# First attention: probabilities times values in split float32r passes, with turned probability tiles read out of PSUM in three groups

## What is computed

```python
# 16 heads of 64, 2 groups of keys and values, 3 branches: compressed (c), selected (s), window (w)
p_s = masked_softmax(s_s, mask_s)
o_s = einsum('bghqm,bgqmd->bqghd', p_s, v_s)
p_w = masked_softmax(s_w, mask_w)
o_w = einsum('bghqk,bkgd->bqghd', p_w, v_w)
o = gc[..., 0:1] * o_c + gc[..., 1:2] * o_s + gc[..., 2:3] * o_w
```

## The kernel before

| engine | turn u before |
|---|---|
| PE | transposes of u-1; scores of u+1; pieces of u; values of u-1 |
| ACT | (high part of two heads, u mod 4 = 1); expo of u; copy of bank 7 if unit u-1 ended a tile; turned block 2 of u-1; queries; split_hi |
| DVE | queries; maxima of u; scaling of u-1; turned blocks 0, 1, 3 of u-1; split_lo; (low part of two heads) |

## Time and profile before

### The profile page before, as it was taken

How to read it: one execution, slowest core, us unless ns; L and a number is a source line. 1 busy time by engine, 2 the same in 40 slices (tenths; PEclk the granted TensorE clock), 3 DMA queues, 4 the chain that set the end, 5 groups by cost and what they waited for, 6 DMA issues and landing times.

```text
span 2089.5 us, 23598 instructions
## 1 busy us (share of the span) xinstructions
PE 1837.3 (88%) x8490; PEld 1468.4 (70%) x8490; DVE 1019.7 (49%) x1657; ACT 775.2 (37%) x1358; POOL 41.2 (2%) x57
## 2 busy tenths in 40 slices
PE   5897599999888799998989978888997997798987
PEld 4777577777667688886767775557874666577966
DVE  5234466566545565663234335664363234534654
ACT  3122144443322455552132125554253442315651
POOL 0001000000000000000000000000000000000001
PEclk8898599999989899999999998898997778898998
DMA  7320001111233233332322230010321011211111
GB/s 181 90 74 27 0 29 43 60 60 48 91 101 121 60 100 100 83 89 81 101 75 81 85 102 1 21 41 21 116 82 40 21 41 37 70 61 41 41 41 40
DMA packets 157156, 135.74 MB, mean 65 GB/s; under 512 B 9744, under 2 KB 151440, under 8 KB 156944
## 3 DMA queue, kind: packets, MB, share of 16 engines
q1 hardware_dynamic: 154032, 126.89, 20.4%
q0 software_dynamic: 1600, 5.24, 0.7%
q10 hardware_dynamic: 1440, 2.50, 0.4%
HBM read 127.28 MB, written 7.34 MB: 64 GB/s over the span
## 4 chain that ended last, share of the span: by engine, by line
PE 77%; DVE 12%; issue 4%; ACT 3%; DMA 2%; SPq 2%; DVEq 0%; ACTq 0%
PE bank L294 18%; PE bank L295 17%; PE bank L296 17%; PE bank L992 3%; PE bank L963 2%; PE bank L976 2%; DVE wlo L287 2%; PE bank L2108 1%; PE bank L476 1%; PE bank L883 1%; PE bank L2472 1%; ACT whi L280 1%; DVE ssn L443 1%; PE bank L1674 1%; PE bank L2094 1%
## 5 line engine op out<-in xcount | busy, mean ns | idle before, releaser
L294 PE MATMUL bank<-hh,whi 128*128 128x512 f32 (+2 forms) x1104 | 450.1, 408 | 37.2 <-DVE hl L415 20.3
L295 PE MATMUL bank<-hl,whi 128*128 128x512 f32 (+2 forms) x1104 | 439.7, 398 | 0.0
L296 PE MATMUL bank<-hh,wlo 128*128 128x512 f32 (+2 forms) x1104 | 439.1, 398 | 0.0
L280 ACT ACTIVATE whi<-wraw 128x2048 fp32r<-128x2048 f32 x112 | 213.9, 1911 | 398.1 <-PE bank L296 388.2
L287 DVE TENSOR_TENSOR wlo<-wraw,whi 128x2048 fp32r<-128x2048 f32 x112 | 256.2, 2288 | 199.3 <-ACT whi L280 197.9
L294 PEld LDWEIGHTS bank<-hh,whi 128*128 128x128 f32 (+2 forms) x1104 | 211.2, 191 | 98.9 <-issue 25.6
L296 PEld LDWEIGHTS bank<-hh,wlo 128*128 128x128 f32 (+2 forms) x1104 | 211.3, 191 | 48.0
L295 PEld LDWEIGHTS bank<-hl,whi 128*128 128x128 f32 (+2 forms) x1104 | 212.0, 192 | 43.3 <-issue 1.7
L1016 DVE COPY pt<-bank 128x128 f32<-128x128 f32 (+2 forms) x96 | 42.6, 469 | 105.6 <-PE bank L976 105.5
L294 PE MATMUL bank<-ah,whi 128*128 128x512 f32 x192 | 77.1, 402 | 12.3 <-DVE al L2607 8.5
L1026 ACT ACTIVATE pr<-bank,nm 128x128 f32<-128x128 f32 (+3 forms) x128 | 66.2, 529 | 45.8 <-DVE nm L1082 45.7
(11 more groups left out here) (354 smaller groups left out, 3106.1 us busy)
## 6 DMA issues: line engine op xcount, KB each, us to landing
wraw<-in_w_in_a_dram SPq DMA_DIRECT2D x52, 512.0 KB, 4.5
wraw<-in_w_up_dram SPq DMA_DIRECT2D x42, 512.0 KB, 4.7
wraw<-in_w_in_dram SPq DMA_DIRECT2D x34, 512.0 KB, 4.7
wraw<-in_w_in_c_dram SPq DMA_DIRECT2D x18, 512.0 KB, 4.4
wraw<-in_w_down_dram SPq DMA_DIRECT2D x16, 512.0 KB, 4.3
wraw<-in_w_out_a_dram SPq DMA_DIRECT2D x16, 512.0 KB, 4.3
aside<-stage POOLq DMA_DIRECT2D x20, 256.0 KB, 2.3
w<-in_cmp_w_dram SPq DMA_DIRECT2D x4, 1024.0 KB, 12.6
```

Of the source, the lines that this page charges most:

```text
L280: act.activation(whi[:, p], wraw[:, p], ACT.Copy).then_inc(w_hi_done, 1)
L294: pe.matmul(out, ws[0], hs[0], start=first, stop=False)
L295: pe.matmul(out, ws[0], hs[1], start=False, stop=False)
L296: return pe.matmul(out, ws[1], hs[0], start=False, stop=last)
```

## The change

The values are kept as a high part and a low part side by side (`vhl`, 64 columns high, 64 low) for each branch and group, as the 128 columns of weights. The probabilities are split after the transposes: ACT copies each turned tile from PSUM into `pth` (float32r), DVE subtracts it from the same PSUM tile into `ptl`. Both have one buffer. `values` makes eight float32r matmuls, for each block one with `pth` and one with `ptl`. The upper 64 rows of bank 6 then hold the product with the high values and the lower 64 rows that with the low values, so a head needs the whole bank: bank 6 is emptied after each head (two units) by `out_half` (ACT, rows 64 to 127 into `osum`) and `out_sum` (DVE, adds rows 0 to 63), and after two heads `out_high` (ACT) and `out_low` (DVE) split `osum`. The compressed branch is one float32 matmul for each head, with 64 columns of weights, at the second unit of the head.

The turned tiles are read out in three groups: blocks 0 and 2 (bank 4), block 1 (bank 5), block 3 (bank 5), each with one signal. The order of the queues is new:

| engine | turn u after |
|---|---|
| PE | group 0 and group 1 of u-1; scores of u+1; group 2 of u-1; pieces of u; values of u-1 |
| ACT | high of groups 0 and 1 of u-1; (out_half, u odd); expo of u+1, blocks 0 and 1; high of group 2; expo of u+1, blocks 2 and 3; (out_high, u mod 4 = 1); copy of bank 7 if unit u-1 ended a tile; queries; split_hi |
| DVE | low of groups 0 and 1 of u-1; (out_sum, u odd); maxima of u+1; low of group 2; scaling of u; (out_low); queries; split_lo |

In `block1_kv` the values are written as a high part by ACT and a low part by DVE, where DVE made one copy before, and POOL's clearing of the padding is gone. In all other stages pairs of semaphores were merged into one that counts higher (`n_root` and `n_rec` into `n_inv`, and so on), with the same waits in the same places.

```diff
         def values(pe, u):
             p, e, b = u // 4, u // 2 % 2, u % 2
-            out = bank[6]
-            if u % 4 == 0:
-                if p:
-                    pe.wait_ge(o_out, p)
-                pe.matmul(out[:, :], vc[:, p // 4, p % 2, :], pct[:, p // 2, :], start=True, stop=False)
-            pe.wait_ge(t_act, u + 1)
-            pe.wait_ge(t_dve, 3 * u + 3)
+            out, g, h = bank[6], p // 4, u // 2
+            if b == 0 and h:
+                pe.wait_ge(o_out, h)
+            pe.wait_ge(t_low, 3 * u + 3)
             for j in range(TT):
-                mm = pe.matmul(out[:, P * j:S], vp[:, j, b, c0:c0 + P], pt[:, u % 2, j, P * j:S],
-                               start=False, stop=(u % 4 == 3 and j == TT - 1))
+                for part in (pth, ptl):
+                    mm = pe.matmul(out[:, P * j:S], vhl[:, j, b, g, :], part[:, j, P * j:S],
+                                   start=(b == 0 and j == 0 and part is pth), stop=False, skip_group_check=True)
+            if b:
+                mm = pe.matmul(out[0:HD, :], vc[:, g, h % 4, :], pct[:, p // 2, :], start=False, stop=True,
+                               skip_group_check=True)
             mm.then_inc(pv_done, 1)
...
+        GROUPS = (((0, 0), (2, P)), ((1, 0),), ((3, 0),))
+        def turn(pe, u, n):
+            pe.wait_ge(p_scaled, 4 * u + (2 * n + 3 if n < 1 else n + 2))
+            if u or n == 2:
+                pe.wait_ge(t_low, 3 * u - 2 if n == 0 else 3 * u if n == 1 else 3 * u + 2)
...
             for u in range(UNITS + 1):
                 if u:
-                    turn(pe, u - 1)
+                    turn(pe, u - 1, 0)
+                    turn(pe, u - 1, 1)
                 if u + 1 < UNITS:
                     scores(pe, u + 1)
+                if u:
+                    turn(pe, u - 1, 2)
                 if u < UNITS:
                     pieces(pe, u)
                 if u:
                     values(pe, u - 1)
...
+            def high(u, n):
+                act.wait_ge(t_done, 3 * u + n + 1)
+                if u and n == 0:
+                    act.wait_ge(pv_done, u)
+                for src, to in turned(n):
+                    ins = act.activation(pth[to], src, ACT.Copy)
+                ins.then_inc(t_high, 1)
...
             for u in range(UNITS + 2):
-                if u < UNITS:
-                    for i in range(TT):
-                        expo(u, i)
+                if 1 <= u <= UNITS:
+                    high(u - 1, 0)
+                    high(u - 1, 1)
+                if u % 2 and u >= 3:
+                    out_half((u - 3) // 2)
+                if u + 1 < UNITS:
+                    expo(u + 1, 0)
+                    expo(u + 1, 1)
+                if 1 <= u <= UNITS:
+                    high(u - 1, 2)
+                if u + 1 < UNITS:
+                    expo(u + 1, 2)
+                    expo(u + 1, 3)
+                if u % 4 == 1 and u >= 5:
+                    out_high((u - 5) // 4)
                 ended = range(done_tiles(u - 2), done_tiles(u - 1))
                 for t in ended:
                     act.wait_ge(tiles, 2 * n0 + t + 1)
                     if t:
                         act.wait_ge(spilled, 16 * t)
                     act.activation(stage[:, :], bank[7][:, :], ACT.Copy).then_inc(drained, 1)
-                if 1 <= u <= UNITS:
-                    turned(act, u - 1, 2, t_act, lambda o, s: act.activation(o, s, ACT.Copy))
...
+            def low(u, n):
+                dve.wait_ge(t_high, 3 * u + n + 1)
+                for src, to in turned(n):
+                    ins = dve.tensor_tensor(ptl[to], src, pth[to].bitcast(F32), ALU.subtract)
+                ins.then_inc(t_low, 1)
```

More of the change, by code:

```diff
@@ L639, in _ @@
             split_hi(act, n0 + 3)
+            for half in range(2):
+                act.wait_ge(tiles, 2 * n0 + 5 + half)
+                for j in range(2):
+                    tt = 2 * half + j
+                    ins = act.activation(vhl[:, tt, :, :, 0:HD],
+                                         bank[half][:, IC * j:IC * j + IC].rearrange("p (b g d) -> p b g d", b=2, g=2),
+                                         ACT.Copy)
+                ins.then_inc(v_high, 1)
             split_hi(act, n0 + 4)
@@ L1009, in _, with turned @@
                     values(pe, u - 1)
[L1011 to L1017, removed]
+        def turned(n):
+            return [(bank[4 + (n > 0)][:, c0:c0 + P * (i + 1)].rearrange("p (j q) -> p j q", j=i + 1),
+                     (slice(None), slice(0, i + 1), slice(P * i, P * i + P))) for i, c0 in GROUPS[n]]
         @block.scalar
@@ L1036, in queries_high, with out_half, out_high @@
                 ins.then_inc(q_hi, 1)
+            def high(u, n):
[5 more added lines that the diff above has]
+                ins.then_inc(t_high, 1)
+            def out_half(h):
+                rows = slice(HD * (h % 2), HD * (h % 2) + HD)
+                act.wait_ge(pv_done, 2 * h + 2)
+                if h >= 2:
+                    act.wait_ge(o_low, h // 2)
+                act.activation(osum[rows, :], bank[6][HD:P, :], ACT.Copy).then_inc(o_half, 1)
+            def out_high(p):
+                act.wait_ge(o_out, 2 * p + 2)
+                act.activation(oh[:, p, :], osum[:, :], ACT.Copy).then_inc(o_high, 1)
             queries_high(0)
             act.wait_ge(c_t, 4)
+            for i in range(TT):
+                expo(0, i)
             for u in range(UNITS + 2):
[L1041 to L1044, removed]
-                if u < UNITS:
-                    for i in range(TT):
-                        expo(u, i)
+                if 1 <= u <= UNITS:
[13 more added lines that the diff above has]
+                    out_high((u - 5) // 4)
                 ended = range(done_tiles(u - 2), done_tiles(u - 1))
@@ new lines, in low, with out_sum @@
+            def low(u, n):
[3 more added lines that the diff above has]
+                ins.then_inc(t_low, 1)
+            def out_sum(h):
+                rows = slice(HD * (h % 2), HD * (h % 2) + HD)
+                dve.wait_ge(o_half, h + 1)
+                dve.tensor_tensor(osum[rows, :], bank[6][0:HD, :], osum[rows, :], ALU.add).then_inc(o_out, 1)
@@ L1073, in _, with out_low @@
+            def out_low(p):
+                if p == NH // 2 - 1:
+                    dve.wait_ge(spilled, 16 * (PV_T + GATE_T))
+                dve.wait_ge(o_high, p + 1)
+                dve.tensor_tensor(ol[:, p, :], osum[:, :], oh[:, p, :].bitcast(F32), ALU.subtract).then_inc(o_low, 1)
             queries_low(0)
+            maxima(0)
             for u in range(UNITS + 2):
+                if 1 <= u <= UNITS:
+                    low(u - 1, 0)
+                    low(u - 1, 1)
+                if u % 2 and u >= 3:
+                    out_sum((u - 3) // 2)
+                if u + 1 < UNITS:
+                    maxima(u + 1)
+                if 1 <= u <= UNITS:
+                    low(u - 1, 2)
+                if u < UNITS:
+                    scaled(u)
+                if u % 4 == 1 and u >= 5:
+                    out_low((u - 5) // 4)
@@ L1635, in _ @@
         def _(pe):
-            pe.wait_ge(l_prod, 1)
-            pe.matmul(bank[4][:, 0:2], ones[:, :], lprod[:, :], start=True, stop=True).then_inc(l_sum, 1)
-            pe.wait_ge(l_lam, 1)
+            pe.wait_ge(l_step, 1)
+            pe.matmul(bank[4][:, 0:2], ones[:, :], lprod[:, :], start=True, stop=True).then_inc(l_step, 1)
+            pe.wait_ge(l_step, 4)
             pe.wait_ge(drained, m1)
```

168 lines of the change are left out of this document (71 added, 97 removed).

## The result

| | before | after |
|---|---|---|
| median, us | 2091.66 | 2146.51 |
| lowest, highest | 2075.64, 2093.07 | 2145.45, 2161.06 |
| profiled span | 2089.5 | 2143.7 |

The change makes the kernel slower, by a ratio of 1.0315 (95% interval 1.027 to 1.0361). 2158 was forecast.

What follows compares the result with a forecast made beforehand. PE set the pace before; afterwards its wait for bank 7's copy was to decide. Profiled span 2089.5 + 40 at full clock + 26 for the clock = 2155.5, so median 2158; range 2108 to 2185.

Steps and rivals of the forecast that it cites:

- The copy behind the exponentials: Attention: PE waits for bank 7's copy, now behind exponentials of the same turn, at 19 first pieces of tiles, +62 us.
- three kinds of stop: PE's 19 waits for bank 7: 11 in even turns (32.0 us), 4 at u mod 4 = 3 (14.0), 4 at u mod 4 = 1 (16.0).
- The clock: Attention: 15 of PE's 19 stops drop the clock to 1.2 GHz, 1.7 us each, +26; bounds 0 and 32.
- one stretch of the merge: Profile before: the 5 us after 3.47 us idle had a mean clock share of 0.66, so 1.7 us were lost.
- two rows: Profile before: idle of 3.47 us followed by a clock share of 0.66, idle of 2.85 us by 1.00.
- The row with 2.85 us idle: Profile before: the clock stayed at 1.00 after this idle, taken to speak against every stop costing clock.
- The rest: Attention at full clock: values -27, transpose waits -14, compressed matmul +7, block 3's bank +6, `split_lo` +4, last unit +2.
- The passes: PE's float32r value matmuls in attention: 1.30 us a unit against 2.15, -0.85 in 32 units, -27 us.
- +4 behind `split_lo`: DVE in attention: `split_lo` runs 0.6 to 1.3 us into the next turn behind five short turns, +4 us.
- +2 in the last unit: End of attention: no scores or pieces cover the longer chain of copies, +2 us.
- Costs at nothing: Added copies in `block1_kv`, POOL's clearing, semaphore names and the last pair's `out_low` were taken to cost nothing.
- The wait for low copies ahead of the values: PE in attention: values may start at 4.87, but pieces last until 5.78, so covered by 0.9 us.

Runs made afterwards that it cites:

- filled stops: Changed kernel with PE making 12, 15 or 17 unread matmuls before it waits for the copy of bank 7: median 2128.51, ratio to before 1.0172.
- the fifth experiment: Changed kernel with bank 7's copy first in ACT's turn, but group 2 transposed right behind group 1, ahead of the scores: median 2126.73, ratio to before 1.0209.
- the second trace: Changed kernel with bank 7's copy first in ACT's turn, profiled again unaltered: span 2080.7 against 2089.0 before, attention stage 278.3 against 288.0.
- the version with the early copy: Changed kernel with ACT's copy of bank 7 first in its turn, ahead of the high copies: median 2058.99, ratio to before 0.9875.

## Why the prediction was right

- **The copy behind the exponentials, +62.** The difference between filled stops and none is 57.8, or 64.7 with the 6.9 us of shorter waits for low copies counted back. The three kinds of stop were forecast at 2.7, 3.3 and 3.8 us of idle, 58.1 in all; the trace shows 2.6 to 2.7, 3.2 to 3.3 and 4.0 to 4.1, and 56.6 in all. One is out of line, that of unit 31: 1.2 where 3.3 were forecast, since in that turn ACT has no exponentials left to do ahead of the copy.
- **The clock, +26 for 15 falls.** Filling the stops gave back 27.5. The forecast was 15 falls of 1.7; the trace has 18, which makes 1.5 each, and they came at all eight odd stops and at nine of the eleven even ones, where seven were guessed. The price of a fall was taken from one stretch of the merge and the count from two rows, so a sum this close is in part luck. The warning of the Trainium skill ("TensorE: Matmul & The Clock Gate", section "A second HAM failure mode: psum-queue depth-cycling") that small idles of PE between groups keep the clock going up and down came closer to the truth in the fifth experiment than my rows did: there waits of 1.8 us brought the clock to 0.92. The row with 2.85 us idle and no fall was no bound from below.
- **The rest, -22.** With both effects away the stage is 14.4 shorter than before (9.7 in the second trace), so this term was too favourable by 8 to 12. The passes themselves were right (1.31 us measured, 1.30 forecast). What was undersized is the waits for low copies. I counted +4 behind `split_lo` and +2 in the last unit. In the version with the early copy they are 6.9 and 4.9 (3.5 at the transposes, 1.4 at the values), and 3.9 come from late high copies on ACT, which the sum did not have. The compressed matmul, 0.14 longer than its row of before, adds 2.
- **Sum.** -14.4 + 57.8 + 27.5 = 70.9 in the stage, forecast 66. The three measured parts add up by construction, being the steps between four versions. Of the forecast's three terms, the first was 8 too favourable, the second 4 too high and the third 2 too low, so the errors partly cancel.
- **The total, 2158.** It was measured at 2146.5 as the median and 2145.5 to 2161.1 as the range. The forecast took every other stage to be as it was; what it lacked is that the scan has more than one length. To judge by the totals, three of the four executions of after had the short one and three of the four of before the long one. The span of 2155.5 that was forecast lies between the changed kernel's two profiled ones, 2143.7 and 2159.8.
- **Costs at nothing.** The added copies in `block1_kv`, the merged semaphores and the last head pair's `out_low` show no wait of PE on them, and the attention begins at 268.1 where it began at 268.7. The wait for low copies ahead of the values, taken to be covered, comes once, 1.4 us in the last unit.

## What to carry to other kernels

When a queue's order is changed by hand, look for every step that stays where it was: its neighbours have moved. Here the exponentials went one turn ahead, the copy that frees the only bank of a second product stayed behind them, and PE waited for work that was itself waiting for PE in the same turn. A step that frees a buffer belongs ahead of work that does not depend on it; put there, the same change gains 10 to 14 us in the stage in place of losing 71. Two edits that shorten DVE's steps gained another 6 in one trace. And a stop has a second price in the clock, here half of the first.

## What the hardware showed

- A stop of PE costs more than its length. 57.8 us of stops brought a further 27.5 us through the clock; in the changed kernel PE is idle for 67 us of 359 and the clock's mean is 0.90. Matmuls that nobody reads, put in the place of the stops, won the 27.5 back. The clock fell at 17 of 19 stops of mostly 2.6 to 4.1 us, at four of 18 of 0.9 to 1.9 us, and 15 times in a stage with 30 waits of 1.7 to 2.3 us.
- The same program has at least two lengths for the scan of the second block, 110 and 119.5 us, at a clock of 0.86 and 0.78, in two executions that are alike to 0.1 us in the attention; a third, 102.3 at 0.93, was seen in one version. What tips it was not tested. With what follows the scan it moves totals by 14 us, so a change in one stage of this kernel is to be read from that stage, and a median of a few executions is uncertain by 0.7%.
